# Eight modulation chunks move into the first feed-forward, and the next batch into the mixer after it

## The reference

```python
def modulation(cvec, w_mod, b_mod):                       # first network
    m = (jax.nn.silu(cvec) @ w_mod + b_mod)[..., None, :] # w_mod: 1024 x 6144 per layer
    return jnp.split(m, 6, axis=-1)

def trunk_layer(...):
    sh1, sc1, ga1, sh2, sc2, ga2 = modulation(c, w_mod, b_mod)
    sh1c, sc1c, ga1c, sh2c, sc2c, ga2c = modulation(c_ctx[None], w_mod, b_mod)
    u = (rmsnorm(x, g_mix) * (1 + sc1) + sh1) @ w_in
    ...
    x = x + ga1 * mix
    x = x + ga2 * squared_relu_mlp(rmsnorm(x, g_mlp) * (1 + sc2) + sh2, w_up, w_down)
    # the context cx likewise, in layer 0 alone

def second_block(...):
    for l in range(DEPTH):
        mod = (c_act @ w_ada[l] + b_ada[l])[:, None, :]
        shift_a, scale_a, gate_a, shift_f, scale_f, gate_f = jnp.split(mod, 6, axis=-1)
        ...
```

## Time and profile before

| | |
|---|---|
| median of 3 runs | 2060.65 us (2054.01 to 2063.05) |
| the profiled execution, its own time | 2062.21 us, of which the span is 2060.4 us |
| mean granted TensorE clock | 0.901 |
| PE busy | 1817.9 us (88%) |
| DVE, ACT busy | 1160.3 us (56%), 691.5 us (34%) |
| loaded | 306.5 MB at 150 GB/s over the span |

### The profile page before, as it was taken

One profiled execution on the slowest core, in us unless ns is written; L12 is line 12 of the kernel. 1 busy time (PEld: TensorE's weight loads), 2 busy tenths in 40 slices (PEclk: granted clock), 3 DMA queues, 4 the chain that ended last, 5 costly groups with the idle time before them and its releaser, 6 DMA issues.

```text
span 2060.4 us, 25840 instructions
## 1 busy us (share of the span) xinstructions
PE 1817.9 (88%) x10564; PEld 1460.7 (71%) x10564; DVE 1160.3 (56%) x1915; ACT 691.5 (34%) x883; POOL 116.5 (6%) x97
## 2 busy tenths in 40 slices
PE   5998987989999998979789979885999798859997
PEld 2775654768888887746579967444999684649996
DVE  2475455564454455654667664558665645486654
ACT  2423333241312223433343433342443233424431
POOL 1010002010000001100100000003000000030000
PEclk7998767999999999978899989887999999579999
DMA  8324455122322322344345536761564458215642
GB/s 317 122 83 164 164 205 184 41 103 82 110 94 82 121 66 95 130 164 164 113 167 181 204 131 227 273 239 50 176 198 162 154 213 298 70 49 177 198 163 89
DMA packets 172086, 310.26 MB, mean 151 GB/s; under 512 B 3232, under 2 KB 60576, under 8 KB 171328
## 3 DMA queue, kind: packets, MB, share of 16 engines
q1 hardware_dynamic: 168304, 295.03, 41.3%
q10 hardware_dynamic: 3376, 12.01, 1.7%
q0 software_dynamic: 288, 1.57, 0.2%
HBM read 306.50 MB, written 2.10 MB: 150 GB/s over the span
## 4 chain that ended last, share of the span: by engine, by line
PE 70%; DVE 17%; issue 5%; ACT 5%; DMA 2%; POOL 1%; DVEq 0%; ACTq 0%; SPq 0%; POOLq 0%
PE bank L503 52%; PE twin L503 14%; DVE arena L1059 4%; PE bank L512 4%; DVE ring_r L1059 3%; ACT arena L1689 2%; ACT arena_r L1689 2%; DMA ring<-in_w_mod 1%; DVE arena L1624 1%; DVE arena_r L1059 1%; POOL rs L1982 1%; DVE params L1059 1%; DMA ring<-in_w_in 1%; DVE params L1489 1%; DVE arena L1139 1%
## 5 line engine op out<-in xcount | busy, mean ns | idle before, releaser
L503 PE MATMUL bank<-arena_r 128*128 128x512 f32 (+2 forms) x2016 | 665.5, 374 | 4.7 <-DVE params L1505 4.4
L1059 DVE TENSOR_TENSOR ring_r<-ring,arena_r 128x4096 fp32r<-128x4096 f32 (+5 forms) x90 | 380.2, 4225 | 242.2 <-ACT arena_r L1689 242.1
L503 PEld LDWEIGHTS bank<-arena_r 128*128 128x128 f32 x2016 | 385.1, 191 | 74.1 <-DVE params L1505 5.1
L1689 ACT ACTIVATE arena_r<-ring 128x4096 fp32r<-128x4096 f32 (+5 forms) x92 | 322.6, 3507 | 339.4 <-PE bank L503 294.0
L503 PE MATMUL bank<-arena_r,actT_r 128*128 128x512 f32 (+5 forms) x768 | 267.5, 388 | 27.8 <-DVE ring_r L1059 17.4
L1689 ACT ACTIVATE arena<-bank 128x256 f32<-128x256 f32 (+6 forms) x236 | 109.0, 462 | 521.9 <-PE bank L503 411.9
L503 PE MATMUL twin<-actT_r,arena_r 128*128 128x256 f32 x1408 | 255.2, 284 | 0.5 <-DVE actT_r L1059 0.4
L503 PEld LDWEIGHTS twin<-actT_r,arena_r 128*128 128x128 f32 x1408 | 220.6, 193 | 1.0 <-DVE actT_r L1059 0.9
L503 PE MATMUL bank<-ring_r,arena_r 128*128 128x512 f32 x560 | 219.2, 391 | 0.0
L503 PE MATMUL bank<-ring_r,actT_r 128*128 128x512 f32 (+5 forms) x576 | 216.0, 375 | 0.0
L503 PE MATMUL twin<-actT_r,ring_r 128*128 128x256 f32 x704 | 199.6, 284 | 0.0
(11 more groups left out here) (165 smaller groups left out, 1804.4 us busy)
## 6 DMA issues: line engine op xcount, KB each, us to landing
ring<-in_w_mod SPq DMA_DIRECT2D x24, 2048.0 KB, 8.2
ring<-in_w_ada SPq DMA_DIRECT2D x24, 2048.0 KB, 8.0
ring<-in_w_gate_up SPq DMA_DIRECT2D x44, 1024.0 KB, 7.4
ring<-in_w_down SPq DMA_DIRECT2D x20, 2048.0 KB, 7.9
ring<-in_w_up SPq DMA_DIRECT2D x16, 2048.0 KB, 7.8
ring<-in_w_out SPq DMA_DIRECT2D x8, 2048.0 KB, 8.1
ring<-in_w_down SPq DMA_DIRECT2D x8, 1792.0 KB, 7.5
ring<-in_w_in SPq DMA_DIRECT2D x6, 2048.0 KB, 8.9
```

What stands on the lines that cost most here:

```text
L503: ins = nc.tensor.matmul(out_, lhsT, rhs, start=start, stop=stop)
L1059: return v.tensor_tensor(o, x, y, op)
L1689: return nc.scalar.activation(o, x, func, **kw)
```

## The change

Batches keep their sizes and their contents. What moves is where they are filled and, with it, where their loads stand in the one list:

- Batch 2 (eight chunks: the last four of layer 1 of the first network, and the first four of the second network) leaves the mixer of layer 1. In layer 0's feed-forward, one chunk stands behind each pair of up chunks and one behind each pair of down chunks.
- The first eight chunks of batch 3 (twelve chunks) take its place in the mixer of layer 1. The last four stay where the first four were, in the second network's layer 0, ahead of its attention; there are none between its 32 units.
- The columns of batch 2 are made beside the first projections of layer 1 instead of at the end of its mixer.
- Batches 1 and 4 stay.

```diff
+BESIDE1 = [16, 8]
+BESIDE2 = [4, 8]
+UP_FILLS = [8, 0]
 def loads():
...
+    for l in range(L):
+        ins = [("in1", l, c) for c in range(len(CH1)) if (l, c) != (0, 0)]
+        early = 2 - (l == 0)
+        out += ins[:early] + [("par1", l, 0)] + ins[early:] + take(BESIDE1[l])
+        out += [("out1", l, h) for h in range(2)]
+        for q in range(4):
+            m = UP_FILLS[l] // 8
+            out += [("up1", l, 2 * q + i) for i in range(2)] + take(m)
+            out += [("down1", l, 2 * q + i) for i in range(2)] + take(m)
+    for l in range(L):
+        ins = [("in2", l, c) for c in range(len(CH2))]
+        out += ins + [("par2", l, 0)] + take(BESIDE2[l])
...
 # PE, attend
-                if i < fills1(l):
+                if i < BESIDE1[l]:
                     fill()
 # PE, mixer1
-                assert not due
-                mod_columns(l + 1)
+                if l == 0:
+                    assert not due
+                    mod_columns(1)
 # PE, layer1
-                due.extend(batch(l + 1))
+                due.extend(batch(1 if l == 0 else 3))
...
+                    if l == 1 and j == 1:
+                        mod_columns(2)
                     beside_in1(l, j)
...
+                if l == 0:
+                    due.extend(batch(2))
                 for q in range(4):
                     for c in (2 * q, 2 * q + 1):
...
+                    if l == 0:
+                        fill()
                     for half in range(2):
...
+                    if l == 0:
+                        fill()
                 through()
 # PE, layer2
-                due.extend(batch(L + l + 1))
+                if l > 0:
+                    due.extend(batch(L + l + 1))
 # DVE, mixer1
-                mod_columns(l + 1)
+                if l == 0:
+                    mod_columns(1)
 # DVE, layer1
+                    if l == 1 and j == 1:
+                        mod_columns(2)
                     beside_in1(l, j)
 # ACT, attend
-                if i == fills1(l):
-                    sums(l + 1)
+                if l == 0 and i == BESIDE1[l]:
+                    sums(1)
 # ACT, layer1
+                    if l == 1 and j == 0:
+                        sums(2)
                     beside_in1(l, j)
```

More of the change, by code:

```diff
@@ L81, in vectors, with take @@
     return 2 if i == 0 else 1
+BESIDE1 = [16, 8]
+BESIDE2 = [4, 8]
+UP_FILLS = [8, 0]
 def loads():
     out, mods = MODS[:NFIRST - 1] + [("in1", 0, 0)] + MODS[NFIRST - 1:NFIRST], MODS[NFIRST:]
[L87 to L101, removed]
+    def take(m):
+        got = mods[:m]
+        del mods[:m]
+        return got
+    for l in range(L):
[10 more added lines that the diff above has]
+        out += ins + [("par2", l, 0)] + take(BESIDE2[l])
+        out += [("out2", l, h) for h in range(2)]
+        out += [("up2", l, c) for c in range(F2 // 256)]
+        out += [("down2", l, c) for c in range(2 * len(HC2))]
+    assert not mods
     return out
@@ L158, in pairs1 @@
     return [(2 * s + q, hp, 256 * s) for s in range(2 if l < L - 1 else 1) for q in range(TS) for hp in range(4)]
-def fills1(l):
-    return BATCHES[l + 1]
 UNITS2 = [(kind, h, q) for q in range(TS) for kind, n in (("fox", 4), ("moba", 4), ("mla", 8)) for h in range(n)]
```

## The result

The changed kernel takes **2126.55 us** (median of 4 runs, 2124.8 to 2127.34) against 2060.48 for the kernel before in the same comparison (4 runs, 2054.01 to 2063.05): 1.0324 times as long, with a 95% interval of 1.03 to 1.0349. The forecast was 2116, with a range of 2092 to 2136. The profiled execution took 2126.25 us, of which the span is 2124.4, at a mean clock of 0.889 (before: 2062.21, 2060.4 and 0.901). So both spans can be set against each other: +64.0.

What follows compares the result with a forecast made beforehand. PE was busy 88% of the span, saturated in layer 0's feed-forward. Feed-forward +66.3, layer 1's mixer 0, second network's mixer -11: +55.3 on 2062.2, so 2117.5, or 2116 us as a median; range 2092 to 2136.

Steps and rivals of the forecast that it cites:

- rival A: The main forecast: all terms as summed, 2116 us, own range 2109 to 2125; chance 0.64.
- C: Rival: loads land later than 7.8 us, 1.75 more on each of eight, +14, so 2130; chance 0.11.
- the clock: Layer 0's feed-forward: the clock falls in each of seven down-chunk stalls, costing 1.7 us each, between nothing and 1.9.
- the stalls: Layer 0's down chunks: late loads make PE stand 4.8 us in four first chunks, 6.3 in three second ones.
- the fills: Layer 0's feed-forward: seven of eight added fills paid at 1.75 us, 12.3 us; the eighth hidden in the norms' wait.
- The second mixer: Second network's layer 0 mixer loses eight fills: -11 us; 128-key units -13.5, 256-key units slower by 3.7.
- The last chunk: Last second down chunk of layer 0's feed-forward: later split end delays the norms, +4 us (+4.4 or +0.5 by landing).
- The up chunks: Layer 0's feed-forward: loads equally late but no stall, as PE needs a bank only at T+21.8; 3.5 us of cover.
- Rival B: The stalls are there but the clock falls in none or few of them: +43.4, so 2104; chance 0.16.
- Layer 1's mixer: First network's layer 1: eight fills before and after, same size, columns moved: 0, between -1.5 and +1.5 us.
- the case in which fills come out whole: Second network's layer 0, 128-key units: five fills come out at 3.5 us each on the lower clock, -17.5.
- D: Rival: not slower, late loads stay hidden behind DVE's split in down chunks; 2062, or 2050; chance 0.06.

Runs made afterwards that it cites:

- Experiment 1: Kernel before, with weight loads in layer 0's feed-forward waiting for the chunk two places back instead of three, no chunk moved: 2123.48 us, ratio 1.0305.
- experiment 4: Changed kernel with DVE's split in layer 0's down chunks moved from the head of the work to behind the second token tile: 2070.59 us, 1.0049.
- experiment 5: Changed kernel with DVE's split in layer 0's down chunks moved behind the first token tile: 2072.74 us, 1.006.
- experiment 7: Experiment 1 plus 32 useless thin matmuls on constants in the middle of each down chunk of layer 0: 2113.75 us, 1.0271.
- Experiment 2: Kernel before plus eight sets of 16 thin matmuls on a constant at the new fill places in layer 0's feed-forward, nothing loaded: 2074.67 us, 1.0069.
- Experiment 8: Kernel before, with four fills of the second network's layer 1 moved from behind 128-key units to behind 256-key units: 2047.7 us, 0.9944.
- experiment 9: Kernel before, with seven of eight products left out of seven fills among the second network's layer 0 units, loads kept: 2052.47 us, 0.9955.
- experiment 11: Experiment 4 with the second network's four layer 1 unit fills and layer 0's four early fills moved among their 256-key units: 2064.43 us, 1.0019.

## Why the prediction was right

The measured 2126.55 lies within the stated range, but above rival A's own 2109 to 2125 and nearer to C's 2130 than to A's 2116. What happened is A's mechanism all the same, with three of its terms too small: the clock by 5.4, the stalls by 2.6 and the fills by 2.6. The second mixer gave 1.4 less than forecast. The last chunk, 1.8 too high, and the start of the stage, which I had put at nothing and which ran 2.1 shorter, took some of that back; that part is luck.

**The ring loses a slot, and DVE's split turns that into a stall.** Right, in place, releaser and size. First down chunks: 4.8 us forecast, 4.71 to 6.13 measured, 20.6 in all against 19.2. Second: 6.3 forecast, 6.25, 6.26 and 7.59 measured, 20.1 against 18.9. What is over comes from the two loads of 9.12 and 9.21 us where I had 7.8. Experiment 1 shows that late loads suffice, experiment 4 that they hurt only because the split stands ahead of the bank's read: with loads as late and the split two tiles later, PE never stops. The up chunks had the slack that the prediction gave them.

**The clock.** The fall came in all seven stalls. The size was off: 1.7 us forecast for each, 11.9 in all, and some 17 measured, as the two blocks behind a resumption take 1.7 to 2.95 us more than 10.9. The upper bound of 1.9 was too low. It was read from a case in which the lower level lasted 3.4 us; here it lasts 6.8 in six of the seven stalls, and PE works in 4.0 to 6.1 of them. Only behind the last stall was it 3.4. This is the largest error of the sum. The Trainium skill, "TensorE: Matmul & The Clock Gate", section "HAM oscillation — how this bites in real kernels", has every tile behind a wait start on the lower clock. By that rule all stalls pay, and the trace agrees for the seven of 4.7 to 7.6 us: 0.50 behind each. The stalls of 0.5 to 1.3 us in experiment 5 had no fall behind them. Rival B is refuted by the trace, and experiment 7 puts a price on most of it: some 11.7 us of clock with five of the seven falls gone, where the prediction had 11.9 between itself and B.

**The last down chunk.** 4 us forecast, 2.2 measured. I had chosen 8.3 us for its load, since it had a row; the load landed after 5.70, nearer to the proportion to its bytes, by which I had +0.5.

**The fills.** Seven at 1.75 us were forecast; from the start of a fill to the next chunk it is about 2.1, 14.9 in all. Experiment 2 gives the part alone: +13. The eighth lay in the wait for the norms.

**Layer 1's mixer**: nothing forecast, +0.3 for the layer.

**The second network's mixer.** -11 forecast, -9.6 measured: -13.4 for the short units (my estimate by steps was -13.5) and +3.8 for the long ones (I had +3.7). I had gone 1.2 beyond the sum of the two, towards the case in which fills come out whole; that addition was wrong. Experiment 8 shows the same step from the other side. Two things make the -9.6 look better than it is. It is taken from the longer form of the kernel before; against the shorter one (62.9) it is -4.4. And the units of layer 1, at which the prediction did not look, take 67.9 us in the changed kernel and 67.7 to 67.9 in experiments 4, 5 and 9, the others in which the fills among layer 0's units are gone or hollow while layer 1's stay; in all kernels with both sets of fills in their old places they take 63.8. In the changed kernel PE does 48.0 us of its work there at the lower clock, against 40.2 before.

**Sum.** Forecast +55.3, measured +64.0 between the profiled executions: clock +5.4, fills +2.6, stalls +2.6, last chunk -1.8, second mixer +1.4, start of the stage -2.1, layer 1 and the rest +0.9. These add up to +9.0 against a difference of 8.7; the 0.3 that are over I put to the clock's term, which is read from the two blocks behind each resumption (17.3 in all) and may overlap with others.

**Rivals.** C, later landings, happened in part: two of the seven loads in question, 2.6 us in stalls and not 14. D, loads hidden, is refuted for this order of DVE's work; experiment 4 is the kernel in which it holds, and it still isn't faster. The Trainium skill, "Perfetto Trace Analysis", section "Optimization Strategy", says that interleaving regimes may improve a kernel where the contended engine changes over time. The trace does not bear it out here. Transfers were not what the mixer paid for (experiment 9), and where they went PE had no time to spare: with every stall removed the move is worth -9.6 + 14.9, a loss of 5.3, and experiment 4 shows +5.9 between the profiled spans and +8.9 between the medians (2070.59 against 2061.67).

**What stays open**: why some loads took 9.1 to 9.2 us, and why the clock falls more often in one execution than in another with the same fills, which gives the second network's units their two lengths (68.1 or 62.9 us in layer 0).

## What to carry to other kernels

A ring of slots is as deep as its order of loads lets it be: a stream put in at every third place of a three-slot ring takes a slot for itself, and every other load goes out a chunk later. Whether that costs anything is decided by what stands ahead of the oldest bank's read in the engine that empties it; split the next weights behind the reads that PE waits for, and the lateness is hidden. Before work is moved into a stretch where TensorE never rests, look for stretches where it waits or runs at its lower clock anyway: four fills among the 256-key units of layer 1 cost nothing, four ahead of layer 0's attention less than nothing, and seven in the feed-forward 2.1 us each.

## What the hardware did that I had not expected

- Once the clock had fallen within a stall, the lower level mostly lasted 6.8 us (488.2 to 495.0, and the same for the falls at 518.9 and 628.1) though PE resumed 1.5 us into it and then worked without a pause. Behind the last stall, where it fell just as PE resumed, it lasted 3.4 us. In the kernel before the like case had 3.4 us. A stall of 4.85 us so cost some 7.5.
- Useless matmuls in a wait made a kernel faster: 2113.75 against 2123.48 us, and 410.1 against 417.8 us for the feed-forward alone (experiment 7).
- Taking fills away from a stretch with waits made that stretch slower, as the clock there went from 1.00 to 0.60 (experiment 11).
- A modulation load issued about a microsecond behind a weight load landed after 12 to 13.6 us, the weight load ahead of it after 7.6 to 9.2; only the weight load is on the chain.
